# A thirteenth projection unit by seven quarter products, and the first head's first scores moved between its sixth and seventh product

## The reference

```
z = rms_norm(x) @ w_in                # 1024 x 6144: q, two forget gates, i, g of the recurrent
                                      # branch, q, k, v of attention, two 1024-wide gates
a = hgrn2_mixer(...)                  # 4 heads of 128, gated linear recurrence, both directions
b = diff_attention(...)               # 4 heads, two softmaxes each: softmax(q1 k1) - lam softmax(q2 k2)
m = sigmoid(gate_a) * (a @ w_a) + sigmoid(gate_b) * (b @ w_b)
x = x + rms_norm(m @ w_out)           # then a conv FFN, and a gated embedding term
```

## Time and profile before

| | |
|---|---|
| median of 3 runs | 2410.37 us (2409.86 to 2410.99) |
| the profiled execution: its own time, its span | 2410.16 us, 2408.2 us |
| TensorE matmul busy, weight loads busy | 100%, 93% of the span |
| VectorE, ScalarE, GpSimd busy | 76%, 54%, 8% |
| granted TensorE clock, mean | 0.999 |
| the layer's Winograd units (last one) end, heads begin | 223.6 us, 241.7 us (layer 0) |
| heads 1, 2, 3 of layer 0 begin level 0 at about | 306, 369, 432 us |

### The profile page before, as it was taken

The page is one execution under the profiler, slowest core; times in us unless marked ns, Lnnn a source line. Parts: engine busy times, 40 slices in busy tenths (PEclk is TensorE's granted clock), DMA queues, the critical chain, the costliest instruction groups (busy, mean ns, idle before and its releaser), DMA issues.

```text
span 2408.2 us, 40381 instructions
## 1 busy us (share of the span) xinstructions
PE 2398.9 (100%) x16184; PEld 2240.6 (93%) x16184; DVE 1837.6 (76%) x2412; ACT 1311.3 (54%) x2023; POOL 196.8 (8%) x236
## 2 busy tenths in 40 slices
PE   9999999999999999999999999999999999999998
PEld 8999999998999999888889999999989999998887
DVE  7656788764888899978585568886649889999784
ACT  6445666542555556456454456665436555564563
POOL 1001011100200000003110011111001000000031
PEclk9999999999999999999999999999999999999999
DMA  5354444354222233733234544434433133346421
GB/s 185 129 175 141 137 148 134 126 182 145 92 90 90 84 97 129 282 128 118 97 131 131 185 136 141 141 128 155 159 137 110 60 96 95 102 165 238 162 88 62
DMA packets 284673, 320.97 MB, mean 133 GB/s; under 512 B 10436, under 2 KB 216776, under 8 KB 284488
## 3 DMA queue, kind: packets, MB, share of 16 engines
q1 hardware_dynamic: 211680, 171.39, 22.8%
q10 hardware_dynamic: 72808, 147.01, 16.9%
HBM read 253.08 MB, written 65.27 MB: 132 GB/s over the span
## 4 chain that ended last, share of the span: by engine, by line
PE 99%; DVE 0%; ACT 0%; issue 0%; DVEq 0%; POOLq 0%; POOL 0%; ACTq 0%
PE ps L909 23%; PE ps L1192 15%; PE ps L1397 13%; PE ps L1137 11%; PE ps L882 6%; PE ps L1503 5%; PE ps L1120 3%; PE ps L1366 3%; PE ps L1333 3%; PE ps L896 3%; PE ps L1252 3%; PE ps L1089 2%; PE ps L1109 1%; PE ps L1018 1%; PE ps L961 1%; PE ps L1483 1%
## 5 line engine op out<-in xcount | busy, mean ns | idle before, releaser
L2149 DVE TENSOR_TENSOR wlo<-raw,whi 128x1024 fp32r<-128x1024 f32 (+1 forms) x152 | 163.9, 1079 | 55.0 <-ACT whi L3177 55.0
L909 PE MATMUL ps<-hT_hi,whi 128*128 128x384 f32 x608 | 203.1, 334 | 0.0
L909 PE MATMUL ps<-hT_hi,wlo 128*128 128x384 f32 x608 | 203.1, 334 | 0.0
L909 PE MATMUL ps<-hT_lo,whi 128*128 128x384 f32 x608 | 203.1, 334 | 0.0
L3191 ACT ACTIVATE U<-ps 128x384 f32<-128x384 f32 x152 | 74.8, 492 | 223.9 <-PE ps L909 223.9
L1397 PE MATMUL ps<-whi,PH_hi 128*128 128x512 f32 x456 | 179.0, 393 | 0.4 <-issue 0.4
L1397 PE MATMUL ps<-whi,PH_lo 128*128 128x512 f32 x456 | 177.7, 390 | 0.0
L1397 PE MATMUL ps<-wlo,PH_hi 128*128 128x512 f32 x456 | 177.5, 389 | 0.0
L1711 DVE TENSOR_TENSOR wlo<-raw,whi 128x1024 fp32r<-128x1024 f32 (+1 forms) x98 | 102.8, 1069 | 80.2 <-ACT whi L2645 80.0
L1584 DVE TENSOR_TENSOR wlo<-raw,whi 128x2048 fp32r<-128x2048 f32 x53 | 121.2, 2286 | 50.7 <-ACT whi L2469 50.7
L909 PE MATMUL ps<-S_hi,whi 128*128 128x384 f32 x456 | 152.3, 334 | 0.0
(11 more groups left out here) (349 smaller groups left out, 6938.5 us busy)
## 6 DMA issues: line engine op xcount, KB each, us to landing
raw<-w_up_dram SPq DMA_DIRECT2D x88, 512.0 KB
raw<-w_in_dram SPq DMA_DIRECT2D x62, 512.0 KB
raw<-w_down_dram SPq DMA_DIRECT2D x60, 512.0 KB, 4.6
raw<-w_in_dram SPq DMA_DIRECT2D x16, 1024.0 KB
zT<-gst ACTq DMA_DIRECT2D x40, 384.0 KB, 2.5
GT<-zT ACTq DMA_DIRECT2D x16, 768.0 KB, 5.9
pD<-CG ACTq DMA_DIRECT2D x26, 384.0 KB, 2.3
zT<-hn ACTq DMA_DIRECT2D x48, 192.0 KB, 1.9
```

Source lines behind the costliest of these rows:

```text
L909: ins = mm(ps[:, 4 * (j % 2) + bank, 0:TH], quarter(L, W[y], j, (w,))[:, 0, k * P:(k + 1) * P], sum_operand(a, x, k), start=(opens and k = ...
L2149: v.tensor_tensor(lo, x, hi.bitcast(F32), ALU.subtract)\
```

## The change

- `IN_UNITS`, `I1 = 15`: one gate unit, (None, 0), is moved ahead of the last two token units and becomes the thirteenth Winograd unit, number 14. Both token units 15 and 16 are now slots of the heads, and seven gate units are 17 to 23. The whole unit between the Winograd units and the heads is gone.
- `SLOTS`: head 0 gets two slots ahead of level 0 (20 in all), heads 1 and 3 one fewer at level 2 (17 each); head 2 keeps its 18. The sum is 72 as before. `side`, `side_halves` and `side_splits` are not changed.
- The first head's first scores go between P3 and P4 of unit 14; their maximum, the rotation of queries and keys, their high and low parts and two Silus are moved forward; the first diagonal product moves behind the two new slots.
- On ScalarE and VectorE the work of `side(PRE)` moves with it; one load call is moved up; the buffers' turns are renumbered.

```diff
-IN_UNITS = [(0, TOKEN_U), (1, TOKEN_U)] + [(h, u) for h in range(NH) for u in range(3)] + [(2, TOKEN_U), (3, TOKEN_U)]\
-    + [(None, u) for u in range(2 * NH)]
+IN_UNITS = [(0, TOKEN_U), (1, TOKEN_U)] + [(h, u) for h in range(NH) for u in range(3)] + [(None, 0)]\
+    + [(2, TOKEN_U), (3, TOKEN_U)] + [(None, u) for u in range(1, 2 * NH)]
-I0, I1 = 2, 14
+I0, I1 = 2, 15
-SLOTS = ((0, 2, 2, 2, 2, 2, 2, 1, 1, 0, 2, 1, 1), (0, 2, 2, 2, 2, 2, 2, 1, 1, 0, 1, 2, 1),
-         (0, 2, 2, 2, 2, 2, 2, 1, 1, 0, 2, 1, 1), (0, 2, 2, 2, 2, 2, 2, 1, 1, 0, 1, 2, 1))
+SLOTS = ((2, 2, 2, 2, 2, 2, 2, 1, 1, 0, 2, 1, 1), (0, 2, 2, 1, 2, 2, 2, 1, 1, 0, 1, 2, 1),
+         (0, 2, 2, 2, 2, 2, 2, 1, 1, 0, 2, 1, 1), (0, 2, 2, 1, 2, 2, 2, 1, 1, 0, 1, 2, 1))
...
-                        if j == min(DENSE + (first - 2) // 8 + (2 if head == 2 else 3), N_IN - 1):
+                        if j == min(DENSE + (first - 2) // 8 + 2, N_IN - 1):
                             load_qk(L, head)
...  TensorE, in mixers
+                side(PRE)
                 if h == 0:
+                    pe.wait_ge(in_act.sem, in_act.at(L, f"c21_{I1 - 1}"))
+                    pe.wait_ge(in_dve.sem, in_dve.at(L, f"c12_{I1 - 1}"))
                     gla_diagonal(it)
-                side(PRE)
...  TensorE, in in_quarters
                 in_product(L, e, "P3")
+                if e == I1 - 1:
+                    pe.wait_ge(in_act.sem, in_act.at(L, f"c21_{e - 1}"))
+                    pe.wait_ge(in_dve.sem, in_dve.at(L, f"c12_{e - 1}"))
+                    att_scores(L * NH, 0)
...
-                for p in range(8):
-                    if p == 4:
...
-                        att_scores(L * NH, 0)
-                    project(unit(L, I1), p, True, ((0, 7), (6, 6)))
...  VectorE, in mixers
                 if h == 0:
-                    att_max(it, 0)
-                    low(unit(L, DENSE))
                     att_weights(it, 0)
-                side(PRE)
...
-                    if k == 0 and h:
-                        for t in range(TAIL, len(SLOTS[h - 1])):
+                    if k == 0:
+                        side(PRE)
+                        for t in range(TAIL, len(SLOTS[h - 1])) if h else ():
...
-                    elif k:
+                    else:
                         side(k)
...  VectorE, behind the Winograd units
                     else:
+                        att_low(L * NH)
                         low(unit(L, I1))
-                        for n in ("cqk", "sqk", "radd"):
-                            att_rope(L * NH, L, n)
...
+                    if not more:
+                        att_max(L * NH, 0)
                     in_sum(L, e, "c12")
+                    for n in {I1 - 3: ("cqk", "sqk"), I1 - 2: ("radd",)}.get(e, ()):
+                        att_rope(L * NH, L, n)
...  ScalarE
                     in_copy(L, e, "p5")
+                    if not more:
+                        gla_silu(L * NH)
                     in_copy(L, e, "u2")
...
                     else:
+                        gla_silu_gate(L * NH)
...
                     in_copy(L, e, "u3")
+                    if e == I1 - 2:
+                        att_high(L * NH)
...
-                high(unit(L, I1 + 1))
-                copy_out(L, I1, 0, (0, 7))
-                store_out(L, I1, 0)
+                done(lay_dve, L, "slw")
                 att_exponentials(L * NH, 0)
-                done(lay_dve, L, "slw")
                 merge_keys(L * NH, 0)
-                copy_out(L, I1, 1, (6, 7))
```

More of the change, by code:

```diff
@@ L560, in unit @@
             n, half = L * N_UNITS + j, L * ((U_DN + N_UNITS - U_PG) // 2) + (j - (U_PG - U_DN if j >= U_PG else 0)) // 2
-            turn = (j + L + (j >= U_PG)) % 2
+            turn = (j + (j >= I1) + (j >= U_PG)) % 2
             return (n, half, j % 2, turn) if i is None else (n + i * each, half + i * (each // 2), j % 2, turn)
@@ L580, in in_quarter @@
         def in_quarter(L, w, e, names):
-            at = [((PLACE[k] + (e % 2 if k == "B22" else 0)) + 4 * L) % 8 * 512 for k in names]
+            at = [(PLACE[k] + (e % 2 if k == "B22" else 0)) * 512 for k in names]
             return view(w[:], at[0], [[at[-1] - at[0] or 512, len(at)], [1, 512]])
@@ L625, in ring_at @@
         def ring_at(L, n):
-            return (n + 2 * (L + 1)) % 4 * 1024
+            return n % 4 * 1024
         def ring(L, w, n):
@@ L637, in quarter @@
         def quarter(L, w, j, names):
-            at = [((PLACE[k] + (j % 2 if k == "B22" else 0)) + 4 * (L + 1)) % 8 * 512 for k in names]
+            at = [(PLACE[k] + (j % 2 if k == "B22" else 0)) * 512 for k in names]
             return view(w[:], at[0], [[at[-1] - at[0] or 512, len(at)], [1, 512]])
@@ L807, in _ @@
                             load_pair(L, j)
+                    elif h is None and j < I1:
+                        load(unit(L, j), [rows(w_in, L, 0, KD, 8 * HW + u * 256 + b * P, P) for b in range(2)])
                     elif h is None:
@@ L1289, in _ @@
                     in_quarters(L, e)
-                pe.wait_ge(in_act.sem, in_act.at(L, f"c21_{I1 - 2}"))
-                pe.wait_ge(in_dve.sem, in_dve.at(L, f"c12_{I1 - 2}"))
-                for p in range(8):
-                    if p == 4:
-                        pe.wait_ge(in_act.sem, in_act.at(L, f"c21_{I1 - 1}"))
-                        pe.wait_ge(in_dve.sem, in_dve.at(L, f"c12_{I1 - 1}"))
-                        att_scores(L * NH, 0)
-                    project(unit(L, I1), p, True, ((0, 7), (6, 6)))
                 for h in range(NH):
@@ L1984, in _ @@
                 gla_keys(L * NH)
-                att_low(L * NH)
                 gla_queries(L * NH)
@@ L2423, in _ @@
                         first_rstd(L, n)
+                g.wait_ge(in_pe.sem, in_pe.at(L, f"P3{I1 - 1}"))
                 gla_totals(L * NH)
@@ L2751, in mixers @@
                     gla_diagonal(it)
-                    store_out(L, I1, 1)
                 side(PRE)
@@ L2986, in _ @@
                         load_qk(L, 0)
-                gla_silu(L * NH)
-                gla_silu_gate(L * NH)
                 gla_sigmoids(L * NH)
@@ L2993, in _ @@
                 load_v(L, 0)
-                att_high(L * NH)
-                high(unit(L, I1 + 1))
-                copy_out(L, I1, 0, (0, 7))
-                store_out(L, I1, 0)
+                done(lay_dve, L, "slw")
                 att_exponentials(L * NH, 0)
-                done(lay_dve, L, "slw")
                 merge_keys(L * NH, 0)
-                copy_out(L, I1, 1, (6, 7))
                 for h in range(NH):
```

## The result

The changed kernel takes 2433.14 us (median; 2433.04 to 2433.41), the kernel before on the same chip 2410.14: a ratio of 1.0095, 95% interval 1.0078 to 1.0112. The forecast was 2434.0 with a range of 2420 to 2445, slower with a chance of 0.91.

What follows compares the result with a forecast made beforehand. TensorE was taken as the bound everywhere, each wait costing its full length. Per layer 9.7 (splits) + 4.3 (small waits) - 2.1 (saving) = 11.9 us, both layers 23.8, on 2410.16: 2434.0 us; range 2420 to 2445.

Steps and rivals of the forecast that it cites:

- The rival that waits find slack: Heads: new waits fall into idle time of TensorE, so the kernel isn't slower, 2406.0 us; chance 0.07.
- The saving: A feature unit falls from eight slots to seven products, 96 matmuls to 84: 2.08 us per layer.
- the start of the layer: From P3 to level 0: VectorE's 9.4 us hidden behind TensorE's 9.9, taken as 0; nearest bound 2 us.
- The six split pairs: Heads 1 to 3: slots side by side in one entry expose ScalarE's copy between them; 9.7 us per layer.
- 19.0: Unit 19's slot 0, head 1's tail, behind 18.7: its copy waits for ScalarE's sigmoid, 0.67 us.
- 19.4: Unit 19's slot 4, behind 19.3 and the output transposes: between 0 and one copy, taken as 0.4 us.
- rival 2: Heads: ScalarE is earlier than thought, each split costs its copy alone and small waits are gone, 2415.8 us; chance 0.06.
- The small waits: Heads, per layer: waits besides the split pairs, sum 4.3 us, bounds 0 and 7.
- far keys of head 2: Unit 22's low part, 2.28 us, now ahead of `far_up` with slack 0.76: wait 1.52 us.
- values at level 2: Heads 1 and 3, single slots give less cover: values wait for At, 0.39 us in both heads.
- weights at level 3: Head 3: a low part delays the weights as well, wait 0.45 us.
- rival 3: TensorE's clock falls: one slot at 1.2 GHz after each of ten waits per layer, 42 us more, 2476; chance 0.03.

Runs made afterwards that it cites:

- e1: Changed kernel with heads 1 to 3 on the slot table of before and head 0 giving one slot back at levels 3 and 4: 2408.47 us, ratio 0.9992.
- e5: Changed kernel with one slot more in head 1's last entry and one fewer at head 3's level 4: 2419.87 us, ratio 1.004.
- e4: Changed kernel with the first head's first scores behind P4 instead of between P3 and P4: 2436.87 us, ratio 1.011.
- e6: Changed kernel with VectorE making unit 22's low part right behind head 2's far keys' factor: 2434.37 us.
- e10: e3 with unit 22's low part moved ahead of the queries of head 3's level 0 on VectorE: 2430.69 us.
- e3: Changed kernel with VectorE making unit 22's low part at head 3's level 0, not in head 2 ahead of the far keys: 2437.26 us.
- e9: e3 with unit 22's low part one instruction earlier on VectorE, ahead of the copy of head 3's level 0: 2434.53 us.

## Why the prediction was right

**The bound.** Right: the steps, not the busy share, said that TensorE had no idle time in the heads. Each new wait was paid in full, and removed ones came back in full (e1, e5). The rival that waits find slack is out. The Trainium skill, Perfetto Trace Analysis, Identifying the Most-Contended Engine, judges TensorE's headroom by MFU (the share of peak arithmetic) and by weight-load busy time; by the second, 93% would have left 168 us of room. Here it left none: thirteen waits a layer went into the time one for one, so in this kernel that share was no measure of room.

**The saving**, 2.08 per layer: its matmuls are gone (24 in all). In e1, where the splits are gone, the stage of layer 0 is 0.6 shorter. The rest is given back: in head 0, 0.59 at the key transposes (288.99 to 289.70, less 0.12), 0.42 at the output transposes (301.55 to 302.14, less 0.17) and 0.2 at the weights of level 5, and 0.2 at the weights of head 1's first two levels. The prediction had the first of these, at 0.5, and not the second, which the changed kernel doesn't show. e4 shows that the start of the layer was hidden by the order, as worked out.

**The six split pairs.** All six stand where the count of slots put them, and none elsewhere:

| slots | predicted | measured (step less 0.173) |
|---|---|---|
| 18.3, 18.4 | 1.31 | 1.15 |
| 19.7, 20.0 | 2.02 | 1.37 |
| 20.3, 20.4 | 1.31 | 1.15 |
| 20.7, 21.0 | 1.77 | 1.60 |
| 21.3, 21.4 | 1.85 | 1.68 |
| 21.7, 22.0 | 1.41 | 1.27 |
| together | 9.7 | 8.2 |

Two things were mis-sized. Each slot was priced at 2.08, but its first pair of matmuls, behind another form, takes 0.44 and not 0.35. The timeline of TensorE, changed kernel, slot 19.7:

```profile
380.59 0.60 PE L1139 MATMUL ps<-hT_hi,whi 128*128 128x384 f32 x2
381.03 0.51 PE L1139 MATMUL ps<-hT_hi,wlo 128*128 128x384 f32 x2
```

That 0.1 explains most of the 0.15 missing at five places. At 19.7 the row used for ScalarE's end came from a level in which ScalarE itself waits for VectorE; in the changed kernel the merged keys and the maximum that ScalarE waits for end 0.5 earlier against the slot's start. TensorE had stood shortly before (19.0, 19.4) while VectorE had not; that this is the reason is argued, not tested. So rival 2, an easier pace, was real, but worth 0.5 at one place and not everywhere.

**The small waits.** Predicted 4.3, found 4.4: far keys of head 2 1.50 (predicted 1.52), of head 0 0.59 (0.5), 19.0 0.60 (0.67), 19.4 0.51 (0.4), values at level 2 0.44 in each of heads 1 and 3 (0.39), weights at level 3 0.36 (0.45). What e6 and e10 change is the reading of the largest. The prediction set it down to `far_up` and its slack of 0.76, and 2.28 - 0.76 fits partly by luck. Behind the start of the slot ahead of the transposes the factor ends 3.60 in the changed kernel and 1.88 in e10. So the low part pushes it by 1.7 and not by 2.28, as VectorE would otherwise have stood 0.35 for ScalarE's squares, and the slack left without it is 0.3 and not 0.76.

**The sum.** 8.2 + 4.4 - 2.1 = 10.5 per layer, and 11.7 was measured. Most of the rest stands directly behind the stops, and the prediction had no term for it: the first step of a split pair's second slot takes 0.28 (339.35 to 339.63) and not 0.173, 0.65 over the six, and the step behind each late value product 0.21 (325.97 to 326.18) and not 0.11. About 0.3 is left in smaller steps without a cause of their own. So the forecast of 11.9 is nearer than its terms were: splits 1.5 too dear, and 1.2 not seen. That these nearly cancel is luck.

**The clock.** It stayed full in the heads of the changed kernel, so rival 3 was rightly small here, but its mechanism exists: e3 and e9 show it behind longer stops.

## What to carry to other kernels

In a program with a fixed order on each engine, a double buffer that is filled in counted slots has a phase: shift the count by one and the last slot of one half and the first of the next fall side by side, so that the copy between them is exposed. Write the sequence out before changing a count; here the table that starts head 2 at an odd slot cost 24.7 us against one that keeps step (e1), and one slot more ahead of head 2 took back 13.3 (e5). And where an engine off the bound works through a stretch without a gap, moving its work within that stretch only changes which consumer waits; take it out of the stretch, and look at who needs it in its new place. Where a view names one engine for a wait on several, check in the program which result is needed, and when it ended.

## What the runs showed of the hardware

- A stop of TensorE of up to 1.7 us in the heads, followed by full work, left the granted clock at 1.00 throughout the heads of the changed kernel, and one of 1.8 us (e6) did so too. One of 3.1 us (e3) was followed in both layers by about 3.4 us at the 1.2 GHz level, beginning 1.2 to 1.3 us after work had resumed; the cost was 1.6 us. One of 2.24 us (e9) did so in layer 1 and not in layer 0 of the same execution. So the length of a stop alone does not decide it, and what else does stays open.
- Two waits of 0.7 to 0.9 us each, 2 us apart (e4, both layers), left it full as well.
- The busy share of weight loads went from 93% to 92%, and that of matmuls from 100% to 99%, for a loss of 23.2 us: neither of these shares shows waits of this size, but the steps do.
- Behind a stop the first step of 384 columns took 0.28 us and not 0.173, at each of the six split pairs; behind another form and without a stop it took 0.26.
